# Products that nobody reads, made by TensorE ahead of four waits of the first block

## The reference

```
h  = rms_norm(x, g_mix)
z  = h @ w_in                      # q, k, v, gates, gla q/k/v, decay, r, two mixing gates
k_cmp, v_cmp = compress_blocks(k_c, v_c)   # two small products, gelu between; then rope on k_cmp
o_nsa = softmax over k_cmp, chosen blocks, window
o_gla = gated linear attention in chunks
mix   = sigmoid(gate_a) * (o_nsa @ w_proj_nsa) + sigmoid(gate_b) * (o_gla @ w_proj_gla)
x1 = x + mix @ w_out
x2 = x1 + mixture_of_experts(rms_norm(x1, g_ffn))
```

## Time and profile before

| | us |
|---|---|
| median of 3 runs | 1320.51 |
| the three runs | 1320.12, 1320.51, 1325.48 |
| the profiled execution, its whole time | 1319.86 |
| its span, first to last instruction | 1318.0 |
| TensorE busy in it | 1213.5 (92%) |
| mean granted clock of TensorE | 0.973 |

### The profile page before, as it was taken

How to read it: one execution, slowest core, us unless ns; L and a number is a source line. 1 busy time by engine, 2 the same in 40 slices (tenths; PEclk the granted TensorE clock), 3 DMA queues, 4 the chain that set the end, 5 groups by cost and what they waited for, 6 DMA issues and landing times.

```text
span 1318.0 us, 18104 instructions
## 1 busy us (share of the span) xinstructions
PE 1213.5 (92%) x6996; PEld 754.1 (57%) x6996; DVE 459.7 (35%) x1021; ACT 420.3 (32%) x804; POOL 220.3 (17%) x327
## 2 busy tenths in 40 slices
PE   7996999798999999999898999998999999999996
PEld 6775756465752324333434332532898677799775
DVE  3565233443330001212222210202555554445554
ACT  4553233243320001013323100201442554444772
POOL 3004265200010000001201000000540213201450
PEclk9998888899999999999999999999999999999999
DMA  9656187544449999999999999999552122656400
GB/s 366 203 165 232 47 312 241 189 148 132 134 126 411 410 409 409 408 370 410 409 409 398 408 406 406 398 410 373 186 172 81 49 81 81 189 180 189 130 18 32
DMA packets 97036, 333.64 MB, mean 253 GB/s; under 512 B 10416, under 2 KB 10672, under 8 KB 96816
## 3 DMA queue, kind: packets, MB, share of 16 engines
q1 hardware_dynamic: 96944, 332.41, 68.1%
HBM read 331.32 MB, written 1.05 MB: 252 GB/s over the span
## 4 chain that ended last, share of the span: by engine, by line
PE 68%; DMA 17%; DVE 5%; ACT 3%; POOL 2%; issue 2%; SPq 1%; DVEq 0%; POOLq 0%; ACTq 0%
PE ps L455 24%; DMA w<-in_w_gate 7%; DMA w<-in_w_up 6%; PE ps L1777 6%; PE ps L2320 5%; PE ps L507 4%; PE ps L2372 3%; DMA w<-in_w_down 3%; PE ps L787 3%; PE ps L799 2%; PE ps L929 2%; PE ps L816 2%; PE ps L1343 2%; SPq L3034 1%; PE ps L2348 1%
## 5 line engine op out<-in xcount | busy, mean ns | idle before, releaser
L2320 PE MATMUL ps<-w,vT 128*32 128x512 f32 x1024 | 194.6, 601 | 14.0 <-DMA w<-in_w_gate 7.2
L439 ACT ACTIVATE ab<-w 128x1024 fp32r<-128x1024 f32 (+2 forms) x117 | 121.9, 1050 | 186.1 <-PE ps L455 184.7
L449 DVE TENSOR_TENSOR ab<-w,ab 128x1024 fp32r<-128x1024 f32 (+2 forms) x96 | 118.5, 1241 | 156.7 <-ACT ab L439 156.7
L2320 PEld LDWEIGHTS ps<-w,vT 128*32 128x32 f32 x1024 | 38.7, 108 | 149.8 <-issue 63.0
L455 PE MATMUL ps<-ab,uA 128*128 128x512 f32 x320 | 107.3, 418 | 10.8 <-POOL ab L449 4.2
L1777 PE MATMUL ps<-w,Uc 128*128 128x512 f32 (+1 forms) x224 | 102.8, 606 | 1.8 <-DVE Uc L1921 1.8
L455 PE MATMUL ps<-UA,ab 128*128 128x256 f32 x512 | 92.8, 283 | 0.4 <-POOL UB L572 0.4
L2372 PE MATMUL ps<-w,bT 128*32 128x512 f32 x512 | 78.8, 598 | 10.3 <-ACT bT L2425 5.5
L455 PE MATMUL ps<-ab,UA 128*128 128x512 f32 (+1 forms) x288 | 87.8, 386 | 0.5 <-POOL UB L572 0.5
L455 PEld LDWEIGHTS ps<-UA,ab 128*128 128x128 f32 x512 | 80.1, 192 | 1.3 <-POOL UB L572 1.2
L455 PEld LDWEIGHTS ps<-ab,uA 128*128 128x128 f32 x320 | 63.2, 201 | 27.4 <-POOL ab L449 4.7
(11 more groups left out here) (517 smaller groups left out, 1905.4 us busy)
## 6 DMA issues: line engine op xcount, KB each, us to landing
w<-in_w_gate SPq DMA_DIRECT2D x128, 512.0 KB, 10.8
w<-in_w_up SPq DMA_DIRECT2D x128, 512.0 KB, 11.7
w<-in_w_down SPq DMA_DIRECT2D x128, 512.0 KB, 11.7
w<-in_w_ada SPq DMA_DIRECT2D x48, 512.0 KB, 7.1
w<-in_w_c SPq DMA_DIRECT2D x48, 512.0 KB, 4.4
w<-in_w_m SPq DMA_DIRECT2D x16, 512.0 KB, 4.9
w<-in_ab_out_w SPq DMA_DIRECT2D x16, 512.0 KB, 8.1
w<-in_w_out SPq DMA_DIRECT2D x8, 512.0 KB, 5.3
```

Of the source, the lines that this page charges most:

```text
L439: e.activation(sp.a(j), w.v, ACT.Copy).then_inc(sp.whole, 1)
L449: e.tensor_tensor(sp.b(j), w.v, sp.a(j).bitcast(F32), ALU.subtract).then_inc(sp.parts[j % NAB], 1)
L2320: ins = e.matmul(t.ps[o, :], ve[:, p % 2, 2 * c + k, o], w.v[:, k, :], start=c + k == 0, stop=c + k == 4)
```

## The change

A function is added that makes n products of the identity with 256 columns of a constant, each into columns 0 to 255 of the bank that TensorE is going to fill next. Each begins a new sum (`start=True`), and the real product that follows begins a new one too, so nothing is left of them. They raise no semaphore. At places 1 to 3 they stand after the `free` of that bank and ahead of the wait: 10, 7 and 10 products. At place 4 there are 2 before the wait for the mixture and 3 between the transposes and the wait for `uA` and `uB`. At place 1 the taking of the bank moves ahead of the waits. The last wait of place 4 moves from the program into `pe_lin_steps`.

```
+        def pe_idle(e, t, n, x):
+            for _ in range(n):
+                e.matmul(t.ps[:, 0:256], ident, x, start=True, stop=True)
+        LEV = cst[:, const_o["lev"][0]:const_o["lev"][0] + 256]
 pe_lin_steps(..., idle=0, need=()):
+                if c == 0 and idle:
+                    free(e, use_[0])
+                    pe_idle(e, use_[0], idle, LEV)
+                for x in need if c == 0 else ():
+                    e.wait_ge(*x)
                 sp.ready(e, j)
 place 1:
+            t = bank.take(ALL, "sm")
+            free(e, t)
+            pe_idle(e, t, 10, bP[:, 0, 0:256])
             e.wait_ge(lower, 4)
             S1.ready(e, j)
-            t = bank.take(ALL, "sm")
-            free(e, t)
 place 2:
-            m10 = pe_lin_steps(e, S1, "m10", uA, uB, 512, range(2), range(4), TWO)
+            m10 = pe_lin_steps(e, S1, "m10", uA, uB, 512, range(2), range(4), TWO, 7)
 place 3:
                     free(e, t)
+                    pe_idle(e, t, 10, LEV)
                     e.wait_ge(kcr_ready, 1)
 place 4:
+            t = Use(*[x[ALL.at % 8] for x in (bank.ps, bank.full, bank.evac)], bank.n[ALL.at % 8] + 1)
+            free(e, t)
+            pe_idle(e, t, 2, LEV)
             e.wait_ge(mix_done, 4)
             (the transposes mxT)
-            for x in bank["mxT"]:
-                e.wait_ge(x.evac, x.n)
             for c in range(2):
-                pe_lin(e, S1, f"out{c}", uA, uB, 512, range(2))
+                for _ in pe_lin_steps(e, S1, f"out{c}", uA, uB, 512, range(2), idle=3 if c == 0 else 0,
+                                      need=[(x.evac, x.n) for x in bank["mxT"]] if c == 0 else ()):
+                    pass
```

More of the change, by code:

```diff
@@ L456, in three, with pe_lin_steps @@
             return ins
-        def pe_lin_steps(e, sp, name, A, B, cols, tiles, on_pool=(), ring_=None):
+        def pe_lin_steps(e, sp, name, A, B, cols, tiles, on_pool=(), ring_=None, idle=0, need=()):
             use_ = {i: bank.take(ring_ or ALL, name) for i in tiles}
```

## The result

| | before | changed |
|---|---|---|
| median, us | 1323.27 (1320.12 to 1325.48, 6 runs) | 1312.26 (1307.51 to 1315.26, 6 runs) |
| ratio | | 0.992, 95% interval 0.9895 to 0.9945 |
| profiled execution, us (span) | 1319.86 (1318.0) | 1312.25 (1310.4) |
| mean granted clock of the profiled execution | 0.973 | 0.982 |

The kernel became faster by 0.8%, 1323.27 x (1 - 0.992) = 10.6 us, with an interval of 7.3 to 13.9 us. The forecast was 7.8 us and 1312.7 us; the two profiled executions lie 7.6 us apart. The median of before had been 1320.51 us over the three runs shown first, and is 1323.27 with three more; so a forecast in us that hit the changed kernel's time rests partly on that luck, and the difference is the better number to learn from.

What follows compares the result with a forecast made beforehand. TensorE (68% of the chain, DMA 17%) was taken as the bound, at half clock behind four waits. Gains of 1.4, 2.3, 2.6 and 1.5 us, 7.8 in all, gave 1312.7 us; 8-in-10 range 1308.0 to 1318.0.

Steps and rivals of the forecast that it cites:

- The price of an added product, and what hides it: At the four places, each product takes 0.447 us at full clock, hidden by TensorE's waits, leaving 0.9 to 1.2 us idle.
- Rival D: At places 1 to 3, added products start at half clock and outlast the waits, costing 8.7 us: 1329; chance 0.05.
- rival B: At place 4, transposes count as idle and the clock is not held: sum 6.3 us, 1314.2; chance 0.12.
- The four terms: Slow stretches behind places 1 to 4 shrink by 0.46 of their length: 1.4, 2.3, 2.6 and 1.5 us.
- the signs that the prediction named: Waits of about 1 us, clock 1.00 behind the places, sm's end 1.4 us earlier, experts' first product at about 380.
- Every idle gap left is below the 2.6 us that kept the clock up: Behind all four places the clock stays at 1.00, since a 2.6 us wait for DVE's part had not lowered it.
- Place 1: 1.4 us: Behind the wait ending at 15.5 us, sm's 3.1 us slow stretch shrinks by 1.4 us.
- rival C: From 150 to 270 us the clock falls at other moments, leaving 2.6 to 6.3 us: 1314.2 to 1318; chance 0.20.
- rival A: After place 3, the clock no longer falls under products of 15 columns: 3.1 us more, 1309.6; chance 0.13.
- Does it reach the end?: From place 1 through the experts' stage nothing is fixed in time, so the whole 7.8 us reaches the end.
- Rival C's special case: The experts' stream starts at a fixed time, so nothing arrives at the end: 1320.5 us; chance 0.04.
- The total: Over the whole kernel, the gains at the four places sum to 7.8 us, giving 1312.7 us.

Runs made afterwards that it cites:

- doubled products: Changed kernel with twice as many added products at every place (20, 14, 20, 4 and 6): 1322.76 us, ratio 0.9989 to the kernel before.
- half-sized one: Changed kernel with about half as many added products (5, 4, 5, 1 and 2): 1317.35 us, ratio 0.9958 to the kernel before.
- narrow: Changed kernel with each added product of 256 columns replaced by two of 15 columns: 1322.56 us, ratio 0.999 to the kernel before.
- place 1 alone: Changed kernel with only the ten products of place 1, those of places 2, 3 and 4 left out: 1323.27 us, ratio 0.9999 to the kernel before.

## Why the prediction was right, and where its steps were not

- **The price of an added product, and what hides it.** 0.448 us against 0.447, and waits left of 1.4, 1.0, 0.8 and 0.9 against 1.2, 1.0, 0.9 and 0.9. Shown from the other side by the doubled products. Rival D (an overrun, 1329) is refuted, and rival B with it: place 4 was held.
- **The four terms.** Taken each by itself they came out within 0.1 us, since both the length of the slow stretch and the ratio of 0.46 were read from rows of before. Place 4 is confirmed by taking it away (1.6 us). Of the signs that the prediction named, only sm's end is off: 0.5 us earlier (31.0 against 31.5) and not 1.4, since the late first rise had taken 0.9.
- **"Every idle gap left is below the 2.6 us that kept the clock up" failed as a rule.** One row at 1.00 was taken for a property of a gap's length, though the same rows spoke against it: place 4's own waits were 2.2 us and, ahead of the transposes, 1.5 us, and behind them the clock was 0.50. The 2.6 us gap lowered the clock in the changed kernel, and the half-sized one left 2.3 us at place 2 and lost its clock there. The waits left at the four places, 0.8 to 1.4 us, are below all of these; nothing here says that 2.6 is safe.
- **"Place 1: 1.4 us" failed as a term of the sum.** The piece shrank by just that, and gr's grew by 1.6. Terms were added up as if each wait decided for itself; here filling one changes what happens behind another. The prediction had this as part of rival C (moved stretches), without a place. Why is open. gr's wait ends at nearly the same times in profiles of both kinds (88.49 with the fall, 88.39 without), so its place in the span doesn't tell them apart. Its distance from the clock's first rise comes closer: the wait ends 80.8 to 82.2 us behind the rise in six of the seven profiles with the fall, and 82.8 to 83.7 us in the five without; the doubled kernel, with the fall at 83.8, stands on the other side. So what place 1 does to gr may be no more than to move its wait by the 1.4 us saved, against the moments at which the clock changes; no run moved that wait alone.
- **What made up for it in the profile.** The scores ran at full clock to their end in the first profile (3.67 in place of 5.02), half of rival A; the clock fell behind them all the same, in m01. They took 3.67 us in six of the seven profiles in which place 3 was held and the scores stood unaltered, and 4.85 to 5.02 where it wasn't (before, narrow, place 1 alone), so this gain goes mostly with place 3. The halved kernel, at 3.67 with place 3 slow, and the second profile of the changed one, at 5.57 with it held, are exceptions, so it isn't shown as an effect of the change.
- **"Does it reach the end?"** Mostly: the experts' stream starts 9.6 us earlier, runs at the same rate and ends 8.8 us earlier. Rival C's special case, a fixed start, is refuted.
- **The total.** Four places 7.9, less 1.6 at gr and 0.9 for the late first rise, plus 1.6 at the scores, 0.8 and 1.7 further on, less 0.8 in the experts' stage and 1.2 in the second block: 7.5, beside 7.6 measured between the two spans. Losses of 4.5 us that the sum didn't have cancelled gains of 4.1 that it didn't have either, and some of both are chance. The mechanism was right at each of the four places; that the sum came out to 0.2 us is luck, and place 1, a fifth of it, is worth nothing by itself.
- **Still open.** The comparison by runs gives 10.6 us (7.3 to 13.9), the two profiles 7.6, which is inside that interval. The profiled execution of before was a quick one, 3.4 us under the median of its six runs, and that of the changed kernel stood at its median; this accounts for the difference without another cause. A run's time goes with its mean granted clock: over 39 runs of before, from 1317.59 us at 0.973 to 1332.85 at 0.963, a line through them gives 1.2 us for 0.001. The mean over these runs is 0.9692, over the six of the changed kernel 0.9792, and 0.010 is worth 12 us by that line. In which stretches the runs differ, a profile of one execution can't say.

## What to carry to other kernels

Read the granted clock just behind every wait: a slow stretch of this kernel is worth 0.46 of its length, and it is bought back by wide products that nobody reads, sized at the measured duration so that about 1 us of the wait is left; twice as many cost all that they bring, half as many brought about half of the gain, and products of 15 columns none that could be told. Don't add up such places as if they were independent: fill the next longer wait too, or take each one away in turn and read the later waits' clocks. Profile a kernel twice before a stretch's gain is believed: the scores' was gone in the second profile. Time single places by their pieces of the chain, since runs of one kernel lay up to 18 us apart here and one place is 1.4 to 2.6.

## What the runs showed that was not expected

- With the clock held behind a wait at 15 us it fell behind another at 88 us, in 7 of 7 profiles against 0 of 5 without. The 2.6 us wait itself was the same in all twelve (2.6 to 2.7 us).
- A fully busy TensorE lost its clock under products of 15 columns and kept it when a product of 256 columns stood ahead of every second one (1.00 over 7.0 us).
- The clock's first rise came 4.7 to 7.7 us after the start, at 6.84 and 7.66 us in two executions of the same kernel. The later one costs: the first ten rows took 7.23 us with the rise at 6.84 and 6.31 with the rise at 4.99.
- Transposes of 128 x 128 in float32 held the clock at all four places as products did.
